# Attention of the first block in rounds of two units with four score banks, transposes in the dense banks

## The chip, the core and the metric

One core of a Trainium2 chip runs the whole program. The metric is the device time of one execution in microseconds (us), from the first to the last instruction and what lies around them.

## The reference

Two transformer blocks of two layers each work on a sequence of 512 positions and 1024 features, all in fp32. A layer of the first block does this:

```python
h = rmsnorm(x, norm_g[layer])
u = h @ w_in[layer]                       # split into q, k, v, gates of A, B, C
ya = forgetting_attention(qa, ka, va, log_sigmoid(fa + b)) * silu(za)   # 4 heads, causal, decay
yb = dilated_mixture_attention(rope(qb), rope(kb), vb) * silu(zb)       # 6 heads, 3 dilations
yc = banded_attention(rope(qc), rope(kc), vc, 127, sinks) * silu(zc)    # 6 heads, window 128
merged = sigmoid(ga)*(ya @ w_br_a) + sigmoid(gb)*(yb @ w_br_b) + sigmoid(gc)*(yc @ w_br_c)
x = x + merged @ w_out[layer]
```

The second block has a layer with differential attention under a relative position bias and a multi-scale pooling ("smoothing") branch, and one with a gated convolution. In each follow a cross attention to 256 memory positions and an MLP with a squared ReLU. A last rmsnorm ends the program.

## The kernel before

Everything is feature-major: x is kept as 8 tiles of 128 features by 512 positions. A dense product keeps fp32 accuracy by splitting each operand into a rounded high part and the rest: per group of 128 features, three fp32r matmuls (high by high, low by high, high by low; lines 333 to 335, and 359 to 361 or 881 to 883 where the positions are the stationary side). Eight groups are one gemm of 128 output features, and it fills one PSUM bank. Attention products (scores in line 534, values in line 622, transposes in line 602) are plain fp32 matmuls, scores and values on half of the array each for the two heads of a unit.

Weights come packed, 128 by 1024 for a gemm, through four raw buffers (`fetch`, line 201). ScalarE writes the high part (`round_hi`), VectorE the low part (`rest_lo`), which also issues the fetch four weights ahead. `ahead` keeps this two to three weights in front of the gemm.

The order on each engine is that in which the Python program emits operations. Generators yield after each group of a gemm. `drive(main, fill, num, den)` runs the attention of one kind as `main` and spreads the dense work of the next kind, `fill`, between its yields, num/den steps for each yield. `later(f, n)` puts a step off by n calls of `flush`.

A unit of attention is a pair of heads and one or two blocks of 128 queries. "forget" (A) has 6 units, "mix" (B) 9 and "sink" (C) 6 in each layer. In step i `attention` emits norm(i-1), values(i-2) and scores(i), yields, then turn(i-1), the transposes of the probabilities, and yields again. Scores take two PSUM banks (SB), transposes two others (PTP), values one (OB), dense gemms three (G). After the scores VectorE adds the bias and takes the maximum, ScalarE the exponential; `norm` divides by the sum on VectorE; after `turn` ScalarE copies the transposed tile to SBUF (PTb), from where `values` reads it.

At the start the first weight, the vector gv and x (four pieces of 512 KB) are loaded in that order; four squares of x for the norm are taken on GpSimd and four on ScalarE. `norm_end` and `stage` put the steps of a norm at given groups of the dense stream; evictions are held back until the last of them.

In the second block the relative bias is loaded from DRAM with a skew and then turned over by a product with a flip matrix (line 1145). Each pooling group has a weight chunk of its own. The cross attention is `cross`, its scores are line 1363, values line 1413 and transposes line 1389.

The driving calls of the first block are:

```python
drive(attention(units("forget", ...), gate_y(...)), gens_B(tokB), 98, 16)
drive(attention(units("mix", ...), gate_y(...)), gens_C(tokC), 138, 22)
drive(attention(units("sink", ...), gate_y(...)), gens_D(), 112, 16)
```

Of the kernel before, what the change touches and what calls it, by code (L numbers as in the profile page):

```python
# [14 lines left out]
NRAW, NHI, NLO, NTMP, NTMX = 4, 4, 3, 5, 5  # L15
# [126 lines left out]
def lay_out(nc, A, plan, T):  # L142
# [13 lines left out]
    PTS = Turns([T["PTb"][:, i, :] for i in range(2)])  # L156
# [44 lines left out]
    def fetch(j):  # L201
        if dry or j >= len(plan):
            return
        n = columns(plan[j])
        dst = raw[:, j % NRAW, 0:n]
        src = A["wts"][128 * offs[j]:128 * offs[j] + 128 * n].rearrange("(p f) -> p f", p=128)
        deps = [W["hi"][j - NRAW], W["lo"][j - NRAW]] if j >= NRAW else []
        W["raw"][j] = Q.dma(SP, lambda e: e.dma_start(dst, src), T["s_w"][j % NRAW],
                            16 * (j // NRAW + 1), *deps)
# [34 lines left out]
    class Weight:  # L244
        def __init__(self, c):
# [6 lines left out]
            self.tok = [W["hi"].get(i), W["lo"].get(i)]  # L252
# [7 lines left out]
        def done(self, o):  # L260
            W["done"][self.i] = o

    fetch(0)
    c_gv = load(gv[:, :], A["gv"])
    c_x = [load(X[:, 2 * i:2 * i + 2, :], A["xT"][:, 2 * i:2 * i + 2, :]) for i in range(4)]
    for j in range(1, NRAW):
        fetch(j)
    c_I = load(ident[:, :], A["ident"])
    c_sv = load(sv[:, :], A["sv"])
    c_tri = load(T["tri"][:, :], A["tri"])  # L270
    c_cos = load(T["cosT"][:, :], A["cosT"])
# [7 lines left out]
    round_hi(0)  # L279
    rest_lo(0)  # L280
    W["h"] = W["l"] = 1
# [41 lines left out]
    def gemm_fm(src, w, parts, evac, N=512, last=True, every=1, n0=0):  # L323
# [3 lines left out]
        for n, (b, t) in enumerate(parts):  # L327
# [9 lines left out]
            o = op(PE, f, w.tok if first else None, src.tok[t], free if first else None)  # L337
# [36 lines left out]
    def drive(main, fill, num, den):  # L374

        acc = 0
        for _ in main:
# [142 lines left out]
    def attention(units, done_pair, late_values=False):  # L520
# [73 lines left out]
        def turn(u):  # L594
            cols = u["cols"]
            u["PT"] = []
            for t, ready in u["P"]:
                bank, free = PTP.take()

# [9 lines left out]
                PTP.give(bank, a)  # L609
# [26 lines left out]
        st["clear"] = op(DV, lambda e: e.memset(T["ST"][:, :, 8:16], 1.0), [f for _, f in STT.idle if f])  # L636
        n = len(units)
# [47 lines left out]
    def to_rope(scale, dst, tok, key):  # L685
        def evac(bank, p):
# [23 lines left out]
            later(rest, 3)  # L710
# [100 lines left out]
    for m in range(8):  # L811
        h = op(AC, act(P0.hi[:, m, :], X[:, m, :], ACT.Copy, scale=gcol("norm0", m)), c_x[m // 2], c_gv)
        P0.tok[m] = [h, op(DV, stt(P0.lo[:, m, :], X[:, m, :], gcol("norm0", m), P0.hi[:, m, :].bitcast(F32),
                                   ALU.mult, ALU.subtract), h)]
    round_hi(1)
    rest_lo(1)
    W["h"] = W["l"] = 2
    for m in range(8):
        if m < 4:
            t, free = TMP.take()  # L820
            sq = op(PO, mult(t, X[:, m, :], X[:, m, :]), c_x[m // 2], free)
        else:
            t, sq = tmp_act_square(X[:, m, :], c_x[m // 2])
        sqa[1] = op(DV, (lambda e, t=t: e.tensor_copy(sqa[0], t)) if m == 0 else add(sqa[0], sqa[0], t), sq, sqa[1])
        TMP.give(t, sqa[1])

# [5 lines left out]
    for l in range(2):  # L832
        if l == 0:
            norm_end((15, 18, 19))
# [77 lines left out]
        def gens_A():  # L912
            yield from projections_A([(QA, qA, "q", 0), (KA, kA, "k", 0)])
            yield from values_A()
            steps = forget()
            rest = projections_A([(QA, qA, "q", 1), (KA, kA, "k", 1)])
            for n, _ in enumerate(rest):
# [6 lines left out]
        def gens_B(tok):  # L924
            for i in range(2):
                yield from gemm_fm(P0, WI(l, ZA + 128 * i), parts8(), to_silu(i, ztok))
# [57 lines left out]
        flush()  # L984
        tokB, tokC = {}, {}
        drive(attention(units("forget", tok, 2, qA, kA, vA), gate_y([0, 1], [0, 1], ztok)), gens_B(tokB), 98, 16)
        drain()
        drive(attention(units("mix", tokB, 3, qB, kB, vB), gate_y([2, 3, 4], [2, 3, 4], ztok)), gens_C(tokC), 138, 22)
        drain()
        drive(attention(units("sink", tokC, 3, qC, kC, vC), gate_y([5, 0, 1], [0, 1, 2], ztok)), gens_D(), 112, 16)  # L990
# [45 lines left out]
    assert len(TB.idle) == 3 and len(PTP.idle) == 2  # L1036
    OB.idle += PTP.idle[1:]
    PTP.idle = PTP.idle[:1]
# [26 lines left out]
    stage((6, one), (11, two), (13, three))  # L1065

    def prepare():
# [9 lines left out]
        lv, flip, oh, rel, frow = T["lvec"], T["flip"], T["oh"], T["rel"], T["frow"]  # L1077
# [3 lines left out]
        c_flip = load(flip[:, :], A["flip"], deps=[hrow])  # L1081
# [35 lines left out]
        c_fr = load(scr, frow[:, :], deps=ft)  # L1117
        yield
# [15 lines left out]
        K["mrow"] = spread(MRC[:, 0:2], K["mcol"], n=2, dst=MRB[:, :], B=SB)  # L1134
        yield
        cs = []
        for h in range(4):

            src = bass.AP(tensor=scr.tensor, offset=scr.offset + 640 * h, ap=[[1, 128], [1, 512]])
            cs.append(load(BI4[h], src, deps=[c_fr, K["sq2"], htok, K["mcol"]]))  # L1140
        for h in range(4):
            for _ in range(3):
                yield
            bank, free = SB.take()
# [3 lines left out]
            SB.give(bank, btok[h])  # L1148
# [73 lines left out]
    def mix(g):  # L1222
        w = Weight(chunk("pool_w", g, halves(0, 1), halves(0, 1)))

        def evac(bank, p):
            t, free = TMP.take()
# [629 lines left out]
```

How the kernel before makes its waits and increments, by code:

```python
    def dma(self, eng, fn, sem, val, *deps):  # L93
        self.op(eng, lambda e: fn(e).then_inc(sem, 16), *deps)
        return Landed(sem, val)
# [9 lines left out]
    def play(self, eng, e):  # L105
        seen = {}
        for o in self.of[eng]:
            need = {}
            for d in o.deps:
                v = need.get(id(d.sem), (0, None))[0]
                need[id(d.sem)] = (max(v, d.val), d.sem)
            for k, (v, s) in need.items():
                if seen.get(k, 0) < v:
                    e.wait_ge(s, v)
                    seen[k] = v
            ins = o.fn(e)
            if o.sig:
                ins.then_inc(o.sem, 1)
# [23 lines left out]
def lay_out(nc, A, plan, T):  # L142
# [1512 lines left out]
                o = send(0, *((0, 3), (3, 3), (6, 2))[m - 3])  # L1655
                if m == 5:
                    SB.give(end[0]["row"][0], o)
    mlp(1, n2)
    drain()
    last_norm(1)
    last_row(1)
    for m, n in ((0, 3), (3, 3), (6, 2)):
        send(1, m, n)
    op(SP, lambda e: e.wait_ge(T["s_o"], 16 * sent[0]))
    return Q, used
```

## Time and profile before

| | us |
|---|---|
| median of 3 runs (2334.63 to 2336.03) | 2334.96 |
| the profiled execution | 2335.33 |
| its span, first to last instruction | 2333.5 |
| TensorE busy | 2305.0 (99%) |
| VectorE busy | 1290.5 (55%) |
| ScalarE busy | 852.4 (37%) |

A matmul's end is modelled, and a busy TensorE is not one at its peak: how dense the stream is shows in the distance between the starts of neighbouring matmuls. Where an engine sits idle ahead of an instruction, the profile names what ended the wait.

### The profile page before, as it was taken

The numbers are of one execution on the slowest core, as the hardware profiler recorded it, in microseconds if no ns is written. First come the engines' busy times: TensorE is split into PE (matmuls) and PEld (weight loads), VectorE is DVE, ScalarE is ACT, GpSimd is POOL, SyncE is SP. The second block draws the span as 40 slices with busy tenths as digits, with TensorE's granted clock in tenths as the row PEclk, the third lists the DMA queues.
The fourth block names the chain that finished last, engine by engine and source line by source line (L and its number), as shares of the span: only waits on it lengthen the run. The fifth ranks groups of instructions, "written<-read, shape, count | busy, mean of one in ns | idle before, by whom it ended". The sixth has DMA issues, their size and how long they took to land.

```text
span 2333.5 us, 28447 instructions
## 1 busy us (share of the span) xinstructions
PE 2305.0 (99%) x11480; PEld 1876.6 (80%) x11480; DVE 1290.5 (55%) x2226; ACT 852.4 (37%) x1416; POOL 18.9 (1%) x18
## 2 busy tenths in 40 slices
PE   8999999999999999999999999999999999999998
PEld 6787778878777887878889888888888887888887
DVE  5855565557556556587545544444655546444445
ACT  4434443333344334255333432232322334332233
POOL 0000000000000000200000000000000000000000
PEclk9999999999999999999999999999999999999999
DMA  4322223323322233224224232323223212222321
GB/s 164 95 87 82 86 68 100 108 74 100 91 81 76 81 97 114 69 91 137 89 84 134 90 100 91 99 91 99 91 92 98 86 50 90 92 99 92 98 92 62
DMA packets 66408, 216.98 MB, mean 93 GB/s; under 512 B 8384, under 2 KB 11712, under 8 KB 66149
## 3 DMA queue, kind: packets, MB, share of 16 engines
q1 hardware_dynamic: 66276, 215.16, 28.9%
q8 instruction: 91, 1.49, 0.3%
q14 instruction: 41, 0.33, 0.0%
HBM read 207.78 MB, written 2.11 MB: 90 GB/s over the span
## 4 chain that ended last, share of the span: by engine, by line
PE 95%; DVE 3%; ACT 1%; POOL 0%; issue 0%; DMA 0%; POOLq 0%; DVEq 0%; SPq 0%; ACTq 0%
PE ps L333 27%; PE ps L335 27%; PE ps L334 27%; PE ps L534 2%; PE ps L622 2%; PE ps L359 2%; PE ps L360 2%; PE ps L361 2%; PE ps L602 2%; PE ps L1363 1%; PE ps L1413 1%; PE ps L423 1%; DVE t_wlo L171 1%; POOL t_UP L168 0%; DVE t_P0L L174 0%
## 5 line engine op out<-in xcount | busy, mean ns | idle before, releaser
L333 PE MATMUL ps<-t_P0H,t_whi 128*128 128x512 f32 x1664 | 672.7, 404 | 11.8 <-DVE t_P0L L174 9.6
L335 PE MATMUL ps<-t_P0H,t_wlo 128*128 128x512 f32 x1664 | 656.9, 395 | 0.0
L334 PE MATMUL ps<-t_P0L,t_whi 128*128 128x512 f32 x1664 | 655.9, 394 | 0.0
L180 ACT ACTIVATE t_whi<-t_raw 128x1024 fp32r<-128x1024 f32 (+3 forms) x396 | 404.6, 1026 | 383.6 <-PE ps L335 334.7
L171 DVE TENSOR_TENSOR t_wlo<-t_raw,t_whi 128x1024 fp32r<-128x1024 f32 (+3 forms) x395 | 466.9, 1185 | 12.3 <-ACT t_whi L180 7.3
L333 PEld LDWEIGHTS ps<-t_P0H,t_whi 128*128 128x128 f32 x1664 | 314.0, 189 | 105.1 <-issue 23.4
L335 PEld LDWEIGHTS ps<-t_P0H,t_wlo 128*128 128x128 f32 x1664 | 313.5, 188 | 73.2
L334 PEld LDWEIGHTS ps<-t_P0L,t_whi 128*128 128x128 f32 x1664 | 313.9, 189 | 69.7 <-issue 2.2
L333 PE MATMUL ps<-t_P1H,t_whi 128*128 128x512 f32 (+1 forms) x932 | 360.7, 387 | 1.7 <-DVE t_P1L L171 1.7
L334 PE MATMUL ps<-t_P1L,t_whi 128*128 128x512 f32 (+1 forms) x932 | 359.5, 386 | 0.0
L335 PE MATMUL ps<-t_P1H,t_wlo 128*128 128x512 f32 (+1 forms) x916 | 355.6, 388 | 0.0
L333 PEld LDWEIGHTS ps<-t_P1H,t_whi 128*128 128x128 f32 x932 | 175.6, 188 | 40.6 <-DVE t_P1L L171 2.5
L334 PEld LDWEIGHTS ps<-t_P1L,t_whi 128*128 128x128 f32 x932 | 175.3, 188 | 37.5
L335 PEld LDWEIGHTS ps<-t_P1H,t_wlo 128*128 128x128 f32 x916 | 172.1, 188 | 37.8
L168 DVE TENSOR_TENSOR t_X<-ps,t_X 128x512 f32<-128x512 f32 (+1 forms) x136 | 89.7, 659 | 159.1 <-PE ps L335 159.0
L180 ACT ACTIVATE t_TMP<-t_TMP 128x512 f32<-128x512 f32 x88 | 55.7, 633 | 293.2 <-DVE t_TMP L174 229.3
L174 DVE SCALAR_TENSOR_TENSOR t_TMP<-ps,t_RB 128x512 f32<-128x512 f32 x64 | 44.2, 691 | 178.4 <-PE ps L335 178.4
L180 ACT ACTIVATE t_Tb<-t_Tb,t_ST 128x256 f32<-128x256 f32 (+3 forms) x128 | 68.3, 534 | 154.7 <-DVE t_ST L177 154.5
L180 ACT ACTIVATE t_P0H<-t_X,t_gv 128x512 fp32r<-128x512 f32 x56 | 39.9, 723 | 143.9 <-DVE t_X L174 130.4
L174 DVE SCALAR_TENSOR_TENSOR t_X<-ps,t_X 128x512 f32<-128x512 f32 x48 | 33.2, 692 | 104.1 <-PE ps L335 104.1
L180 ACT ACTIVATE t_P1H<-t_TMP 128x512 fp32r<-128x512 f32 x88 | 55.7, 633 | 87.1 <-DVE t_TMP L165 47.7
L180 ACT ACTIVATE t_PTb<-ps 128x384 f32<-128x384 f32 (+1 forms) x112 | 55.4, 533 | 62.4 <-PE ps L602 40.2
(242 smaller groups left out, 2410.0 us busy)
## 6 DMA issues: line engine op xcount, KB each, us to landing
t_raw<-in_wts SPq DMA_DIRECT2D x364, 512.0 KB, 3.5
t_raw<-in_wts SPq DMA_DIRECT2D x16, 384.0 KB, 3.0
t_raw<-in_wts SPq DMA_DIRECT2D x4, 520.0 KB, 6.4
t_X<-in_xT SPq DMA_DIRECT2D x4, 512.0 KB, 7.4
t_raw<-in_wts SPq DMA_DIRECT2D x8, 256.0 KB, 2.6
t_TMX<-t_TMX SPq DMA_DIRECT2D x28, 64.0 KB, 2.0
t_TMP<-t_TMX SPq DMA_DIRECT2D x24, 64.0 KB, 2.0
outT<-t_X SPq DMA_DIRECT2D x4, 384.0 KB, 3.1
```

Source lines behind the costliest of these rows:

```text
L168: return lambda e: e.tensor_tensor(o, a, b, ALU.add)
L171: return lambda e: e.tensor_tensor(o, a, b, ALU.subtract)
L174: return lambda e: e.scalar_tensor_tensor(out=o, in0=a, scalar=s, in1=b, op0=f, op1=g)
L180: return lambda e: e.activation(o, a, f, **k)
L333: e.matmul(bank[:, 0:N], wh, xh, start=first, stop=False)
L334: e.matmul(bank[:, 0:N], wh, xl, start=False, stop=False)
L335: return e.matmul(bank[:, 0:N], wl, xh, start=False, stop=end)
L359: e.matmul(out, xh, wh, start=k == 0, stop=False)
L360: e.matmul(out, xh, wl, start=False, stop=False)
L361: return e.matmul(out, xl, wh, start=False, stop=k == 7)
L534: i = e.matmul(bank[:, o:o + n], l, r, start=True, stop=True)
L602: i = e.transpose(bank[:, j:j + 128], t[:, j:j + 128], ident[:, :])
```

## The change

Attention of the first block is emitted in rounds of two units: values of the last round, scores of both new units, two yields, then norm of each, and the transposes of each head as steps of their own. Scores have four banks, transposes use the dense banks, and the probabilities have two more buffers on either side of the transposes. If the second unit of the last round opens a new pair of heads, its values come after the scores.

```diff
-    G = Turns([ps[:, b, :] for b in (0, 1, 2)])
-    SB = Turns([ps[:, b, :] for b in (3, 4)])
-    PTP = Turns([ps[:, b, :] for b in (5, 7)])
-    OB = Turns([ps[:, 6, :]])
+    spare = [ps[:, b, :] for b in (6, 7)]
+    G = Turns([ps[:, b, :] for b in (0, 1, 2)] + spare)
+    SB = Turns([ps[:, b, :] for b in (3, 4, 5)])
+    PTP = Turns([])
+    OB = Turns([])
...
-        def turn(u):
+        def turn(u, which=None, B=PTP):
...
+        if in_rounds:
+            rounds = [units[i:i + 2] for i in range(0, len(units), 2)]
+            for r, now in enumerate(rounds + [[]]):
+                past = rounds[r - 1] if r else []
+                crossing = len(past) == 2 and past[1]["first"]
+                for u in past[:1] if crossing else past:
+                    values(u)
+                for u in now:
+                    scores(u)
+                if crossing:
+                    values(past[1])
+                yield
+                flush()
+                if now:
+                    yield
+                    flush()
+                for u in now:
+                    yield
+                    flush()
+                    norm(u)
+                for u in now:
+                    for j in range(2):
+                        yield
+                        flush()
+                        turn(u, j, G)
+            return
...
-            later(rest, 3)
+            later(rest, 4)
...
-        drive(attention(units("forget", tok, 2, qA, kA, vA), gate_y([0, 1], [0, 1], ztok)), gens_B(tokB), 98, 16)
+        drive(attention(units("forget", tok, 2, qA, kA, vA), gate_y([0, 1], [0, 1], ztok), in_rounds=True), gens_B(tokB), 90, 25)
```

"mix" is driven with 138, 38 and "sink" with 112, 25. Until the first layer's first projections are done the two spare banks serve dense gemms; then bank 6 becomes the output bank and bank 7 the fourth score bank. One gate gemm moves from the fill of "forget" to the projections ahead of it, and the second query projection ahead of the values.

At the beginning the first two weights are loaded and split in halves, x in eight pieces laid out one after the other, with the second half of the first weight behind the second piece. Eleven products of a matrix of ones run on TensorE first. All squares of x are taken on ScalarE, and the norm's steps come later:

```diff
+    def warm(e):
+        for _ in range(11):
+            i = e.matmul(ps[:, 4, 0:128], ones[:, :], ones[:, :], start=True, stop=True)
+        return i
+
+    op(PE, warm, c_ones)
+    split_cut(0, 0)
...
-            norm_end((15, 18, 19))
+            norm_end((19, 21, 23))
```

A weight's `done` now also calls `ahead`. In the second block the bias is copied 128 times in DRAM by DMA and read back with a skew that needs no flip; the row of the memory norm gets three yields between its two steps; the four pooling weights are one chunk, and a pooled product is split straight from PSUM:

```diff
+        c_rep = [load(A["rep"][h], scr[h:h + 1, :].broadcast_to([128, 640]), deps=[c_fr]) for h in range(4)]
...
-            p = op(PE, lambda e, bank=bank, h=h: e.matmul(bank, flip[:, :], BI4[h], start=True, stop=True),
-                   cs[h], c_flip, free)
-            btok[h] = op(DV, lambda e, bank=bank, h=h: e.tensor_copy(BI4[h], bank), p)
...
+            src = bass.AP(tensor=rep.tensor, offset=rep.offset + 128 * 640 * h + 127, ap=[[639, 128], [1, 512]])
+            btok[h] = load(BI4[h], src, deps=[c_rep[h], K["sq2"], htok, K["mcol"]])
```

`drive` has a new argument `lead`, fill steps taken ahead of the first step of `main`: two for the even attention (90, 42 in place of 92, 41) and for both cross attentions. The second cross attention waits five fill steps in place of three before it opens output gemms, and opens a third one, of six groups, before it ends the first two.

## Rows read from the trace of the kernel before

**Rows 1.** The page: busy us of each engine, and one group of VectorE's.
```profile
PE 2305.0 (99%) x11480; PEld 1876.6 (80%) x11480; DVE 1290.5 (55%) x2226; ACT 852.4 (37%) x1416; POOL 18.9 (1%) x18
...
L174 DVE SCALAR_TENSOR_TENSOR t_TMP<-ps,t_RB 128x512 f32<-128x512 f32 x64 | 44.2, 691 | 178.4 <-PE ps L335 178.4
```
**Rows 2.** Waits of TensorE, whole run: us, times, longest us.
```profile
PE ps L1363 <- DVE t_E L174: 2.5, 4, 0.8
PE ps L333 <- DVE t_wlo L171: 2.5, 2, 2.2
PE ps L333 <- DVE t_P1L L171: 1.7, 2, 1.4
```
**Rows 3.** Order of time, TensorE, scores alone: start, us, instruction.
```profile
63.97 0.40 PE L334 MATMUL ps<-t_P0L,t_whi 128*128 128x512 f32 x1
64.20 0.40 PE L335 MATMUL ps<-t_P0H,t_wlo 128*128 128x512 f32 x1
64.53 0.92 PE L534 MATMUL ps<-t_QKV 64*128 64x384 f32 x4
...
65.71 0.39 PE L334 MATMUL ps<-t_P0L,t_whi 128*128 128x512 f32 x1
```
**Rows 4.** Order of time, TensorE, values alone.
```profile
239.05 0.39 PE L335 MATMUL ps<-t_P0H,t_wlo 128*128 128x512 f32 x1
239.38 0.88 PE L622 MATMUL ps<-t_PTb,t_QKV 128*64 128x128 f32 x12
...
240.52 0.39 PE L334 MATMUL ps<-t_YL,t_whi 128*128 128x512 f32 x1
```
**Rows 5.** Order of time, TensorE, values and scores together.
```profile
85.29 0.39 PE L335 MATMUL ps<-t_P0H,t_wlo 128*128 128x512 f32 x1
85.61 0.88 PE L622 MATMUL ps<-t_PTb,t_QKV 128*64 128x128 f32 x12
86.41 0.93 PE L534 MATMUL ps<-t_QKV 64*128 64x128 f32 x8
...
87.62 0.39 PE L334 MATMUL ps<-t_P0L,t_whi 128*128 128x512 f32 x1
```
**Rows 6.** Order of time, TensorE, the first scores of layer 0.
```profile
54.36 1.68 PE L534 MATMUL ps<-t_QKV 64*128 64x128 f32 x8
```
**Rows 7.** Order of time, TensorE, transposes of two units.
```profile
69.63 0.82 PE L602 MATMUL ps<-t_ident,t_Tb 128*128 128x128 f32 x6
...
176.84 1.03 PE L602 MATMUL ps<-t_ident,t_Tb 128*128 128x128 f32 x8
```
**Rows 8.** Order of time, ScalarE, the copies of those transposes.
```profile
71.55 0.85 ACT L180 ACTIVATE t_PTb<-ps 128x384 f32<-128x384 f32 x2
...
177.48 1.09 ACT L180 ACTIVATE t_PTb<-ps 128x512 f32<-128x512 f32 x2 [1.13 <-PE ps L602]
```
**Rows 9.** Stretch of "forget": PE, PEld, DVE, ACT, POOL busy, PEclk, DMA share, GB/s.
```profile
54.00:131.00 77.00, 76.43 (x459) 61.27 (x460) 57.08 (x121) 29.66 (x60) 0.00 (x0) 1.00 0.30 89
```
**Rows 10.** Groups of VectorE, 53 to 125 us: count, busy us, mean ns.
```profile
L174 DVE SCALAR_TENSOR_TENSOR t_Tb<-ps,t_fg,t_M 128x512 f32<-128x512 f32 x3 | 2.2, 748 | 5.7 <-PE ps L534 5.7
```
**Rows 11.** Order of time, the start, all engines.
```profile
7.94 5.08 ACT L180 ACTIVATE t_P0H<-t_X,t_gv 128x512 fp32r<-128x512 f32 x8 [2.59 <-DMA t_X<-in_xT]
8.69 7.81 DVE L174 SCALAR_TENSOR_TENSOR t_P0L<-t_X,t_gv,t_P0H 128x512 fp32r<-128x512 f32 x8 [2.09 <-ACT t_P0H L180]
9.56 0.79 PE L333 MATMUL ps<-t_P0H,t_whi 128*128 128x512 f32 x1 [9.56 <-DVE t_P0L L174]
...
18.01 0.39 PE L333 MATMUL ps<-t_P0H,t_whi 128*128 128x512 f32 x1
```
**Rows 12.** Two stretches of the first gemms, columns as in rows 9.
```profile
9.50:14.90 5.40, 5.34 (x11) 3.32 (x12) 5.40 (x6) 5.40 (x9) 3.80 (x3) 1.00 1.03 407
15.20:20.00 4.80, 4.80 (x22) 3.89 (x21) 4.70 (x7) 3.09 (x5) 0.00 (x0) 1.00 0.94 331
```
**Rows 13.** Order of time, TensorE, one flip product.
```profile
947.93 1.02 PE L1145 MATMUL ps<-t_E,t_flip 128*128 128x512 f32 x2
```

More of the change, by code:

```diff
@@ L251, in __init__ @@
             ahead(i)
-            self.tok = [W["hi"].get(i), W["lo"].get(i)]
+            self.tok, self.late = [W["hi"].get(i), W["lo"].get(i)], {}
+            if i < NCUT and not dry:
+                self.tok, second = ([W["hi"][i][k], W["lo"][i][k]] for k in range(2))
+                self.late = {4: second}
         def hi(self, b, n=1):
@@ L372, in gemm_tm, with drive @@
             finish(bank, o, lambda bank, p, t0=t0: evac(t0, bank, p))
-    def drive(main, fill, num, den):
+    def drive(main, fill, num, den, lead=0):
         acc = 0
+        for _ in range(lead):
+            next(fill)
         for _ in main:
@@ L592, in norm @@
             STT.give(s, o[-1])
-        def turn(u):
+        def turn(u, which=None, B=PTP):
             cols = u["cols"]
-            u["PT"] = []
-            for t, ready in u["P"]:
-                bank, free = PTP.take()
+            u.setdefault("PT", [])
+            for t, ready in u["P"] if which is None else u["P"][which:which + 1]:
+                bank, free = B.take()
                 def f(e, t=t, bank=bank):
@@ L924, in gens_B @@
         def gens_B(tok):
[L925 to L926 removed]
+            yield from gemm_fm(P0, WI(l, ZA + 128), parts8(), to_silu(1, ztok))
             for i in range(3):
@@ L1063, in three @@
         N.row = spread_it(N.diag, dst=RB[:, :], B=SB)
-    stage((6, one), (11, two), (13, three))
+    stage((6, one), (12, two), (15, three))
     def prepare():
@@ L1242, in fill_E @@
         yield from queries(1)
+        w = Weight(tuple(("pool_w", g, (0, 64), (0, 64)) for g in range(4)))
         for g in (0, 2):
-            yield from mix(g)
-            yield from mix(g + 1)
+            yield from mix(w, g)
+            yield from mix(w, g + 1)
             yield from queries(2 + g // 2)
@@ L1296, in rest @@
             TMP.give(t, hs[h])
-        later(rest, 2)
+        later(rest, 3)
         return [o]
@@ L1302, in even_main @@
         yield from attention(eun, head_done, late_values=True)
-        for _ in range(3):
+        for _ in range(4):
             flush()
@@ L1459, in fill @@
                 return
-            for _ in range(3):
+            for _ in range(5):
                 yield
@@ L1472, in cross @@
         if l == 0:
-            drive(main(), fill(), 5, 1)
+            drive(main(), fill(), 5, 1, lead=2)
         else:
-            drive(main(), fill(), 13, 3)
+            drive(main(), fill(), 13, 3, lead=2)
+        if open_:
+            open_.append(wo(2))
+            for _ in range(6):
+                next(open_[2])
         for g in open_:
```

135 lines of the change are left out of this document (81 added, 54 removed).

## The prediction

> **What bounds the kernel now.** I read the busy shares first, then the list of what TensorE waited for, then the stretches, and only then single insertions in order of time. TensorE is busy 99% of the span [rows 1], so the kernel is a queue of matmuls. Waits that the profile can name are few: besides the first start there are 2.5 us each for a rounded weight and for projected queries, and 1.7 us for the last split attention tiles [rows 2]. A gain must therefore come from these waits, from the start, from matmuls that go away, or from time that "busy" hides. The last is there. A dense matmul follows the one before it every 0.23 us [rows 3], but where an attention step is pushed between two of them, the stream loses more than the step's own work. I measure an insertion from the start of the last dense matmul ahead of it to the start of the second one behind it, less two dense steps of 0.23 us. Scores alone cost 65.71 - 64.20 - 0.46 = 1.05 us [rows 3], values alone 240.52 - 239.05 - 0.46 = 1.01 us [rows 4], values and scores together 87.62 - 85.29 - 0.46 = 1.87 us [rows 5]. Together they are 0.19 us cheaper than apart. The rows show why: scores use the array as 64*128, values as 128*64, dense work and transposes as 128*128. Apart there are four changes of shape, together three, so I take a change to cost 0.19 us.
>
> **Rounds of two units.** A layer has 6, 9 and 6 units in its three attentions, and each attention makes two insertions of scores alone, n-2 of values with scores and two of values alone: 6 x 2 + 15 x 3 + 6 x 2 = 69 changes of shape. After, each attention has 3, 5 and 3 rounds: an opening pair of scores (2 changes), then values, values, scores, scores (3 changes, six times a layer), the crossing form values, scores, scores, values (4 changes, once in "forget" and once in "mix"), and values alone at the end (2). That is 6 + 18 + 8 + 6 = 38. Saved: 31 x 0.19 = 5.9 us a layer, 11.8 us in both. Transposes keep the dense shape; cutting each unit's into two insertions I cost at nothing. The first scores of a layer's "forget" lose time too: eight passes take 1.68 us there [rows 6] against 0.93 us elsewhere [rows 5], because the second score bank has just held a spread row that ScalarE still copies. With four banks the fresh one comes third. That gives 2 x 0.75 = 1.5 us.
>
> **What the rounds add.** Two waits, neither in the trace of before. First, turn(u1, 1) now stands directly ahead of the next round's values, with no fill between; ahead there were some six steps. Eight transposes are begun within some 0.8 us (1.03 with the tail of the last), one head's four in 0.40; with ScalarE free the first copy starts 177.48 - 176.84 = 0.64 us after the first transpose, and the two take 1.09 [rows 7, 8]. The second unit's values can thus start about 0.64 + 0.57 + 0.05 = 1.26 us after the transposes began. TensorE is there after 0.40 (transposes) + 0.19 (change) + 0.61 (first unit's values, 86.41 - 85.61 less a change) = 1.20. So with a free ScalarE the first unit's values just cover the copy. With ScalarE behind a weight rounding the copy came 71.55 - 69.63 = 1.92 us after the first transpose, 1.3 late [rows 7, 8]. Between 0 and 1.3 I take 0.3, nearer the prompt row, since the round's exponentials are over by then. Eight such borders a layer; the last round of "mix" has one unit and no cover: 1.26 - 0.59 + 0.3, about 0.95. Sum 2 x (8 x 0.3 + 0.95) = 6.7 us; ends 1.3 and 25. Values of the second unit in a crossing have two score insertions as cover and cost nothing; without that cover they would wait for VectorE's evacuation of the one output bank.
>
> Second, VectorE gets two units' score work in one piece while it is busy 57.08 of 77 us in "forget" [rows 9]. Adding the bias to a head of 512 columns takes 0.75 [rows 10]; with the maximum, of about that length, and the small steps I put a head at 1.9 and the four heads of a round at 7.5 us. Five yields of 3.6 dense steps (12.4 us) stand between the scores and the first transposes; meanwhile dense work with its rope steps brings VectorE some 0.6 us per us, by my estimate. 7.5 + 0.6 x 7.4 (up to the first norm) + 1.4 for that norm is 13.3, so the transposes are due 0 to 3 us before their data in the second round, where rope steps are densest. I take 1 us a layer, 2 us in all; ends 0 and 6. In "mix" and "sink" one step does what "forget" needs three for, and I take nothing. Dense banks: three, each turn takes one and gives it back behind a copy; a dense gemm of 5.5 us lies between an eviction and the bank's next need, so nothing, and 0.5 us per round if VectorE is late.
>
> Attention net: 11.8 + 1.5 - 6.7 - 2 = 4.6 us.
>
> **The start.** TensorE begins at 9.56 us and is through the first gemm at 18.01 [rows 11], though eight groups are 5.5 us of work. It is slow for three reasons: x arrives from 7.9 us on, in pieces of 512 KB behind a whole weight; the low parts take 7.81 / 8 = 0.98 us each while GpSimd squares beside them (0.69 for the like operation elsewhere [rows 1]); and 11 matmuls run in 5.4 us where later 22 run in 4.8 [rows 12]. The view grants 1.00 in both, but the steps say the lower of the two clocks, 1.2 GHz, up to about 15 us. The Trainium skill ("TensorE: Matmul & The Clock Gate", Part 1) has the idle array at 1.2 GHz, released by activity; 11 warm-up matmuls ahead of the data are what that asks for. The change brings the first x behind 0.3 MB instead of 0.6, warms the array and takes the squares off GpSimd. All of x still comes behind the same 2.6 MB: 1.5 MB after 7.9 us, at 407 GB/s [rows 12] by 11.6. Then one copy (5.08 / 8 = 0.63), one low part (0.7) and one group (0.7): the first gemm ends near 14.0, a gain of 4.0. Two more dense banks and the later norm steps should take 0.9 us of small waits in the first 30 us with them. Sum 4.9; ends 2.5 (low parts no faster) and 6.5. ScalarE takes four more squares, 2.1 us, behind the copies, hidden by the second gemm; bare they would delay the norm row.
>
> **The rest.** The four flip products leave. The two passes of one last 1.02 us [rows 13] with the tail that the next matmul overlaps (a dense one lasts 0.40 and is followed after 0.23, so the tail is 0.17): 0.86 of the stream each, 3.4 us in all. The memory row's diagonal is built three yields earlier; I put the wait that this takes away at 0.7, about one VectorE step of that width [rows 1]. Together 4.1, ends 3 and 5. In their place four replicating transfers of 328 KB and four skewed loads run some 35 us ahead of their use. SP holds the weight fetches back while the bias row lands, by my estimate 2 us; raw weights lie more than two gemms ahead, so nothing, 2 us if that cover were gone. One pool weight instead of four small ones and two fill steps ahead: the 2.2 us wait for wlo goes [rows 2]; around it lie shorter waits and slow steps that I estimate at 1.3: 3.5, ends 1 and 4.5. Cross attention: two steps of lead take the waits for queries, 2.5 [rows 2], and a third output gemm covers most of the 1.7 for the split tiles; about 3.5 (ends 2 and 4.5).
>
> **Sum.** 4.6 + 4.9 + 4.1 + 3.5 + 3.5 = 20.6 us off the profiled execution's 2335.3 is 2314.7; the median of the runs is 0.4 lower: **2314 us**.
>
> **Rivals.** (a) The borders don't wait: ScalarE always ready, no burst: 6.7 - 1.3 + 2 = 7 us better, 2307. For it: the copy and the cover are equal to 0.06 us. Against it: ScalarE rounds a weight of 1 us per gemm. (b) The borders wait in full, 0.8 us each and VectorE 3 us a layer: 2 x (8 x 0.5 + 2) = 12 worse, near 2326. (c) The burst decides: VectorE, not TensorE, sets each round. If its two-unit piece makes the first transposes of all 22 rounds 2 us late, that is 44 us against 29 won (the sum without the two waits): 2335 + 15 = 2350, slower. It decides from 1.3 us per round, mean of all. For it: 74% busy in "forget"; against it: 55% over the span [rows 9, 1]. (d) The clock falls again: the groups of the first gemm come every 0.7 to 1 us, so TensorE is partly idle behind the warm-up; at 3 x 5.4 / 11 = 1.47 us a group [rows 12], from 6 us on, the gemm would end at 17.8, 3.8 later than I have it, and the time be 2318. The same page of the Trainium skill has idle gaps bring the low clock back; no row here shows it for gaps that short. (e) The change doesn't act: small waits eat each gain and it stays within 2330 to 2339.
>
> **Numbers.** Own forecast 0.49, (a) 0.14, (b) 0.18, (c) 0.07, (d) 0.07, (e) 0.05. What can be told from no change is about 0.2%, 4.7 us. Faster is all but (c) and (e): 0.88; same 0.05; slower 0.07. The range leaves out (c), (e) and the far ends: 2304 to 2326.
>
> **What would show it.** Attention stretches without the change of clock, score rows of two units in one piece, fewer changes of shape; a wait of TensorE for ScalarE's PTb copy at values, some 0.3 us, 1 at the end of "mix"; the first dense matmul near 6 us and the second gemm near 14; no flip rows; no wait for wlo near 1000 us. Wrong if the values or transposes wait over 1.3 us per round, or if the second gemm starts after 16 us.

## The result and the profile after

The changed kernel takes 2317.1 us (median of 4 runs, 2315.8 to 2318.2) beside 2334.9 us of the kernel before on the same chip: ratio 0.9923, 95% interval 0.9905 to 0.9940, a gain of 17.8 us where 20.6 had been worked out. Its profiled execution took 2317.4 us with a span of 2315.6. TensorE is still busy 99%. The page's busy line and the rows of its list of waits on which the text rests (columns as in [rows 2]):

```profile
PE 2292.8 (99%) x11494; PEld 1882.9 (81%) x11494; DVE 1282.3 (55%) x2217; ACT 859.4 (37%) x1419; POOL 13.9 (1%) x14
```

```profile
PE ps L661 <- ACT t_PTb L182: 4.2, 3, 2.4
PE ps L641 <- DVE t_QKV L176: 2.4, 2, 1.2
PE ps L661 <- ACT t_PTX L182: 1.8, 2, 1.0
PE ps L641 <- DVE t_Tb L176: 1.8, 3, 0.8
...
PE ps L641 <- DVE t_Tb L179: 1.0, 2, 0.5
```

The waits of [rows 2] are gone: none for projected queries, none for wlo, 0.3 us left for the split tiles. New ones stand in their place, at values (L661) and transposes (L641). (t_Tb holds the normalised probabilities, t_PTb and t_PTX their transposed copies; t_PTX is the two buffers that the change adds, all of them behind the transposes.)

Busy TensorE hides where time goes, so I lay the two traces side by side by dense matmuls. Both kernels issue the same 9708 of them; the time at which the n-th starts in the one, less that in the other, is how far the changed kernel is ahead. The gain of each stage, in us, for this kernel and for the experiments told below (each from one profiled execution, against the kernel before). The column "predicted" has the prediction's terms put into the stages: half of the attention net in each layer, and the 0.9 us of small waits in layer 0.

| stage, up to dense matmul | predicted | after | a_old_order | b_no_warm | c_pool_squares | d_border | e_turn_sb | f_spread | g_no_lead | h_all | i_border_spread | j_best | k_flips | l_flips_early |
|---|---|---|---|---|---|---|---|---|---|---|---|---|---|---|
| first gemm, 25th | 4.0 | 3.9 | 3.0 | 3.1 | 0.7 | 3.6 | 3.5 | 3.9 | 3.6 | 3.7 | 1.4 | 4.3 | 1.5 | 1.4 |
| layer 0, 1400th | 3.2 | 3.8 | 2.7 | 3.7 | 3.8 | 5.9 | 5.1 | 3.8 | 3.7 | 3.9 | 4.4 | 7.4 | 3.8 | 3.8 |
| layer 1, 3400th | 2.3 | 1.9 | 0.9 | 1.9 | 1.9 | 4.2 | 3.3 | 1.8 | 1.9 | 2.2 | 2.6 | 5.7 | 2.0 | 1.9 |
| bias and memory row, 3900th | 4.1 | 3.7 | 3.7 | 3.7 | 3.7 | 3.7 | 3.7 | 3.7 | 3.7 | 3.7 | 3.7 | 3.7 | -8.2 | 0.3 |
| even block's attention, 4600th | 3.5 | -1.1 | -1.1 | -1.1 | 0.5 | 0.5 | -1.1 | 1.7 | 0.5 | 1.7 | 0.2 | 1.7 | -1.1 | -0.9 |
| cross attentions, to the end | 3.5 | 5.2 | 5.1 | 5.1 | 5.2 | 5.1 | 5.1 | 5.2 | 1.6 | 5.2 | 5.0 | 5.1 | 5.1 | 5.2 |

A stage that an edit doesn't touch repeats within some 0.2 us from kernel to kernel, apart from the first gemm and the even block's attention, which the text comes to. So the table tells parts apart that are smaller than the spread of whole runs. Five of the six stages are near the prediction or better; the even block's attention is 4.6 us short of it, more than the 3.2 us that the sum lacks.

**The start** answers to [rows 11, 12]: TensorE in order of time, the 22 small matmuls of the warm-up (11 products in two passes), the first dense matmul, a wait for a low part, and the 25th dense matmul; then the stretch of [rows 12] again.

```profile
1.31 5.06 PE L314 MATMUL ps<-t_ones 128*128 128x128 f32 x22 [1.31 <-DVE t_nst L310]
7.15 0.50 PE L370 MATMUL ps<-t_P0H,t_whi 128*128 128x512 f32 x1 [0.77 <-ACT t_P0H L182]
...
9.81 0.50 PE L370 MATMUL ps<-t_P0H,t_whi 128*128 128x512 f32 x1 [0.86 <-DVE t_P0L L176]
...
14.12 0.39 PE L370 MATMUL ps<-t_P0H,t_whi 128*128 128x512 f32 x1
```

```profile
9.50:14.90 5.40, 5.08 (x22) 4.09 (x23) 5.31 (x10) 5.34 (x10) 0.00 (x0) 1.00 1.06 400
```

22 matmuls stand where 11 did, and from the first dense matmul on the steps between matmuls without a wait are 0.23 to 0.34 us, where the kernel before needs 0.43 and more.

**The rounds.** Where they wait: the transposes of the first round of "forget", and the last values of "mix" and "sink" in layer 0.

```profile
69.02 0.52 PE L641 MATMUL ps<-t_ident,t_Tb 128*128 128x128 f32 x3 [0.54 <-DVE t_Tb L179]
...
72.78 0.55 PE L641 MATMUL ps<-t_ident,t_Tb 128*128 128x128 f32 x3 [1.15 <-DVE t_QKV L176]
...
249.41 1.09 PE L661 MATMUL ps<-t_PTb,t_QKV 128*64 128x128 f32 x16 [1.04 <-ACT t_PTb L182]
...
342.05 1.09 PE L661 MATMUL ps<-t_PTb,t_QKV 128*64 128x128 f32 x16 [0.73 <-ACT t_PTb L182]
```

And an ordinary border in "mix", where the prediction had put 0.3 us between the two units' values:

```profile
156.10 0.49 PE L641 MATMUL ps<-t_ident,t_TbX 128*128 128x128 f32 x3
156.52 0.88 PE L661 MATMUL ps<-t_PTb,t_QKV 128*64 128x128 f32 x12
157.23 0.82 PE L661 MATMUL ps<-t_PTX,t_QKV 128*64 128x128 f32 x12
157.99 1.89 PE L573 MATMUL ps<-t_QKV 64*128 64x512 f32 x12
```

The second values start 0.71 us after the first, which is the twelve passes' own time: no wait. The waits are few and long, not many and short. The list of waits gives 2.4 + 1.0 + 1.8 + 1.8 = 7.0 us for both layers (the 2.4 us one at L661 belongs to the even block).

**The even block's attention** is where the forecast failed. TensorE in order of time, then ScalarE and VectorE just before:

```profile
1006.09 0.40 PE L372 MATMUL ps<-t_P0H,t_wlo 128*128 128x512 f32 x1
1008.89 0.94 PE L661 MATMUL ps<-t_PTb,t_E 128*128 128x128 f32 x6 [2.40 <-ACT t_PTb L182]
...
1010.99 0.63 PE L370 MATMUL ps<-t_P0H,t_whi 128*128 128x512 f32 x1
1011.41 0.63 PE L371 MATMUL ps<-t_P0L,t_whi 128*128 128x512 f32 x1
```

```profile
1004.90 1.06 ACT L182 ACTIVATE t_whi<-t_raw 128x1024 fp32r<-128x1024 f32 x1
1007.83 0.63 ACT L182 ACTIVATE t_TMP<-t_E 128x512 f32<-128x512 f32 x1 [1.87 <-DVE t_E L1363]
1008.37 0.47 ACT L182 ACTIVATE t_PTb<-ps 128x384 f32<-128x384 f32 x1
```

```profile
1003.52 0.75 DVE L176 SCALAR_TENSOR_TENSOR t_P1L<-ps,t_gv,t_P1H 128x512 fp32r<-128x512 f32 x1 [1.35 <-ACT t_P1H L182]
1004.18 1.22 DVE L173 TENSOR_TENSOR t_wlo<-t_raw,t_whi 128x1024 fp32r<-128x1024 f32 x1
1005.32 0.74 DVE L176 SCALAR_TENSOR_TENSOR t_P1L<-ps,t_gv,t_P1H 128x512 fp32r<-128x512 f32 x1
1005.98 1.22 DVE L173 TENSOR_TENSOR t_wlo<-t_raw,t_whi 128x1024 fp32r<-128x1024 f32 x1
1007.11 0.68 DVE L1363 COPY t_E<-ps 128x512 f32<-128x512 f32 x1
```

Read backwards: the values wait for ScalarE's copy of the transposes (1008.37); that stands in ScalarE's queue behind a head's square (1007.83), which waits 1.87 us for VectorE's copy of the head (1007.11); and that stands behind two weight roundings and two split tiles. So the pool mixes still bring a burst on. Before, it was wlo that came late, by 2.2 us [rows 2], in a VectorE queue that was full too, though of attention's steps more than of roundings: wlo stood behind a norm (from 998.90 on), the score work of a unit and an eviction.

```profile
998.90 0.18 DVE L577 RECIPROCAL t_ST<-t_ST 128x4 f32<-128x4 f32 x1 [0.78 <-ACT t_Tb L180]
...
1001.84 0.68 DVE L174 SCALAR_TENSOR_TENSOR t_E<-ps,t_RB 128x512 f32<-128x512 f32 x1
1002.43 1.22 DVE L171 TENSOR_TENSOR t_wlo<-t_raw,t_whi 128x1024 fp32r<-128x1024 f32 x1
```

Now roundings and splits hold up an innocent copy for 2.4. Behind it the steps are 0.43 us instead of 0.23, and the row of the stretch shows the clock granted at the lower of its two levels, 1.2 GHz, most of the time (0.57 in the PEclk column; columns as in [rows 9]):

```profile
1010.00:1012.40 2.40, 2.40 (x8) 1.42 (x6) 1.45 (x6) 1.94 (x5) 0.00 (x0) 0.57 0.16 63
```

### The profile page after: what moved, and what is told of

It is laid out like the page before. It is cut to its first block, busy times and chain, and to the rows that moved or that the text cites. A ratio compares the mean times of both kernels' runs of the same rounds, so it can differ in the third digit from the quotient of the medians.

```text
span 2315.6 us, 28450 instructions
## 1 busy us (share of the span) xinstructions
PE 2292.8 (99%) x11494; PEld 1882.9 (81%) x11494; DVE 1282.3 (55%) x2217; ACT 859.4 (37%) x1419; POOL 13.9 (1%) x14
## 4 chain that ended last, share of the span: by engine, by line
PE 94%; DVE 3%; ACT 1%; POOL 0%; issue 0%; DMA 0%; SPq 0%; POOLq 0%; DVEq 0%; ACTq 0%
PE ps L370 27%; PE ps L372 27%; PE ps L371 26%; PE ps L661 2%; PE ps L573 2%; PE ps L396 2%; PE ps L397 2%; PE ps L398 2%; PE ps L641 1%; PE ps L1485 1%; PE ps L1435 1%; PE ps L462 1%; POOL t_UP L170 0%; DVE t_wlo L173 0%; PE ps L948 0%
## 5 line engine op out<-in xcount | busy, mean ns | idle before, releaser
L176 DVE SCALAR_TENSOR_TENSOR t_TMP<-ps,t_RB 128x512 f32<-128x512 f32 x64 | 44.3, 691 | 178.7 <-PE ps L372 178.7
L176 DVE SCALAR_TENSOR_TENSOR t_X<-ps,t_X 128x512 f32<-128x512 f32 x48 | 33.2, 691 | 100.3 <-PE ps L372 100.3
L167 DVE TENSOR_TENSOR t_TMP<-ps,t_RB 128x512 f32<-128x512 f32 x34 | 23.5, 692 | 93.7 <-PE ps L372 93.7
```

Source lines behind the costliest of these rows:

```text
L176: return lambda e: e.scalar_tensor_tensor(out=o, in0=a, scalar=s, in1=b, op0=f, op1=g)
```

## The experiments

All times are medians in us beside 2317.1 of the changed kernel; the kernel before ran beside each (2333.97 to 2335.6). Kernels are called by the first letter of their names where that is plain. An experiment's own runs spread by 0.6 to 5 us, so differences under 2 us are read from the table of stages.

### What the rounds are worth: a_old_order

```
-        if in_rounds:
+        if in_rounds and False:
             rounds = [units[i:i + 2] ...
```
(with the two transpose banks, two score banks and the shares 16, 22 and 16 of the kernel before)

> The change with its first block's attention put back: units one after another, transposes in the two banks of before, two score banks, the old shares of dense work; all else as after. My theory (an array-shape change costs 0.15 to 0.2 us, so the rounds are worth about 1.9 us in each of the two layers at equal dense work): about 3.7 us slower than after, 2320.8 us, with nothing else moved by more than 0.5 us. Rival: the rounds are worth nothing net, since their own waits of 4.0 us a layer eat the saving, and layer 0's gain comes from the earlier start: 2317 us. Rival: the prediction's count of 4.6 us net for both layers: 2321.7 us.

Measured: 2319.7 (2317.9 to 2320.7; ratio to before 0.9935, 0.9922 to 0.9947). That is 2.6 more than with the rounds, but the two intervals overlap; the stages are clearer: 2.7 instead of 3.8 in layer 0, 0.9 instead of 1.9 in layer 1, nothing elsewhere but 0.9 in the first gemm, which the edit doesn't touch (its matmuls went at half rate from 8.7 us on). So the rounds are worth 1.0 to 1.1 us a layer, some 2.1 in all: less than half of the 4.6 forecast and less than my 3.7, which had put down to them 0.9 us a layer that the kernel in the old order has too.

### Waits at the ends of "mix" and "sink": d_border

```
+                if past:
+                    yield
+                    flush()
                 for u in past[:1] if crossing else past:
                     values(u)
```
(shares 28, 43 and 28 instead of 25, 38 and 25)

> The change with one more group of dense products put at each border of two rounds, ahead of the first unit's values (the shares of dense work raised to 28, 43 and 28 so that the amount in each stretch stays). My theory: only three waits a layer are left there (the end of the second stretch and of the third, about 1.0 us each), so some 2 to 4 us in all, 2313 to 2315 us, unless each extra split of a merged run costs two changes of array shape (0.15 us each, 8 borders, two layers: 4.8 us), which would eat it: 2317 to 2319 us. Rival of the prediction: the border waits are the full 6.7 us, so 2310.5 us.

Measured: 2312.9 (2311.6 to 2316.0; ratio 0.9909, 0.9895 to 0.9922). The waits at values in the first block are down to two of 0.3 us, and each layer gains 2.1 to 2.3 us more. But the wait in front of the first transposes of each layer has grown, from 0.5 us to 1.9:

```profile
PE ps L641 <- DVE t_Tb L179: 3.8, 2, 1.9
```

The reason is in the stretch before it; VectorE (third of the busy columns) is full, TensorE is not:

```profile
60.00:69.00 9.00, 7.41 (x33) 5.67 (x31) 8.65 (x21) 5.72 (x15) 0.00 (x0) 1.00 0.17 60
```

But VectorE's share is 8.65 of these 9 us in the changed kernel too, where TensorE has 8.48. What differs is the dense work. The first scores and the first transposes of the layer, in the changed kernel (whose transposes start at 69.02, above) and in d:

```profile
54.10 1.67 PE L573 MATMUL ps<-t_QKV 64*128 64x128 f32 x12
```

```profile
54.41 1.67 PE L573 MATMUL ps<-t_QKV 64*128 64x128 f32 x12
...
69.34 0.52 PE L641 MATMUL ps<-t_ident,t_Tb 128*128 128x128 f32 x3 [1.93 <-DVE t_Tb L179]
```

The chain through VectorE takes 14.9 us in both. A share of 28 in place of 25 hands out fewer dense groups for each yield, so that 48 dense matmuls stand in these 14.9 us in place of 54: 6 x 0.23 = 1.4 us less cover, which is what the wait has grown by. The group at the border was taken out of a stretch that had none to spare.

### Waits of the transposes for a dense bank: e_turn_sb

```
-                        turn(u, j, G)
+                        turn(u, j, SB)
```

> The change with the transposes of the first block written to the score banks, not to the dense ones. Theory: the waits of 1.1 to 1.3 us at the first transposes of a layer are for VectorE's eviction of a dense bank, so they go: 2.4 us faster, about 2314.7 us. Rival: VectorE is late there anyway (the transposes' input, the normalised tile, is 0.5 to 0.7 us late in the turn before), so the wait only changes its name: 2317 us. Second rival: the score banks are now held by the transposes until ScalarE's copy, the first scores of the next round wait at each border (16 borders, up to 0.5 us each): up to 8 us slower, 2325 us.

Measured: 2315.1 (2314.3 to 2315.4; ratio 0.9916, 0.9903 to 0.9930), 1.4 us more in each layer. The wait at L641 for t_QKV (2.4 us, the eviction of a dense bank) is gone, that for t_Tb L179 is unchanged at 1.0, and no score waits in its place. A transpose that borrows a dense bank waits for that bank's eviction; the score banks were free when the transposes came.

### The burst of roundings: f_spread

```
-            yield from mix(w, g)
-            yield from mix(w, g + 1)
-            yield from queries(2 + g // 2)
+            for g in (2 * i - 4, 2 * i - 3):
+                yield from mix(w, g)
+                for _ in range(4):
+                    next(q)
+                    yield
+            yield from q
```

> The change with the pool mixes of the first even block spread: four groups of the queries' dense products between one mix and the next, so that the smoothing's roundings do not come in one burst on VectorE and ScalarE. Theory: the wait of 2.4 us of the values for the copy of the transposes, and the half-rate products behind it (about 10 steps, 0.2 us more each), are due to the burst of weight roundings: they go, 2.4 to 3.5 us faster, 2313.9 to 2314.9 us. Rival: the burst only moves to the next rounding that a product needs, and a wait of 1 us or more stands there under the name of the weight: 2316 to 2318 us.

Measured: 2315.1 (2314.8 to 2315.4; ratio 0.9917, 0.9903 to 0.9930); the even block's stage goes from -1.1 to 1.7. The wait of 2.4 us for the copy is gone, and the matmuls behind it keep their 0.23 us. As the rival had it, part of the wait stands elsewhere, here for a split of a pooled product (the matmul does not read t_P1L; the split is straight from PSUM and gives the bank back):

```profile
1012.65 0.39 PE L370 MATMUL ps<-t_MH,t_whi 128*128 128x256 f32 x1 [0.79 <-DVE t_P1L L176]
```

### Warm-up: b_no_warm

```
-    op(PE, warm, c_ones)
```

> The change without the 11 products of ones ahead of the first dense product. Prediction's step: half-rate steps of 0.43 us come back from 9.56 on as in the kernel before, some 4 us of them (the second product's start at 18.0 instead of 14.1), so 2321 us. Rival: the first products are now paced by the arrival of the input's pieces (0.67 us apart) and the smaller vector work, not by the clock, and half-rate steps hide in that: less than 1 us, 2317 to 2318 us.

Measured: 2317.5 (2316.5 to 2318.4; ratio 0.9929, 0.9914 to 0.9944). The half-rate steps do come back, but only seven of them (the last at 10.5 us), and they stand where the kernel with the warm-up waits for low parts; the first gemm ends 0.8 us later. The rival was right.

```profile
7.77 0.80 PE L369 MATMUL ps<-t_P0H,t_whi 128*128 128x512 f32 x1 [7.77 <-DVE t_P0L L176]
8.37 0.63 PE L370 MATMUL ps<-t_P0L,t_whi 128*128 128x512 f32 x1
...
11.46 0.39 PE L369 MATMUL ps<-t_P0H,t_whi 128*128 128x512 f32 x1
```

### Squares beside the low parts: c_pool_squares

```
+        if m < 4:
+            t, free = TMP.take()
+            sq = op(PO, mult(t, X[:, m, :], X[:, m, :]), c_x[m], free)
+        else:
             t, sq = tmp_act_square(X[:, m, :], c_x[m])
```

> The change with the squares of the first four pieces of the input on GpSimd again. Theory: they stretch VectorE's subtractions for the low parts beside them (0.98 us each before, 0.68 after); P0L of these pieces comes up to 0.3 us later each, the second product's start 0.5 to 1.2 us later: 2317.6 to 2318.3 us. Rival: the pieces arrive 0.67 us apart and bind, so no change, 2317.1 us.

Measured: 2319.4 (2317.6 to 2321.8; ratio 0.9938, 0.9922 to 0.9955), and the first gemm loses 3.2 of its 3.9 us: more than either theory gave. GpSimd's squares stretch VectorE's work beside them, a low part from 0.74 to as much as 1.52 us and a weight's low part from 0.69 to 1.52; TensorE, at half rate from its fourth matmul on, runs dry ahead of 11.70. That matmul, the first of the third group, starts at 9.81 in the changed kernel: 1.9 of the 3.2 us are lost by then, to the late low part. The other 1.3 are lost behind it, where the steps are 0.43 us until 14.4; they are the clock's, and as the text on the start tells below, the clock was low there in executions without GpSimd's squares too.

```profile
5.71 5.38 POOL L167 TENSOR_TENSOR t_TMP<-t_X 128x512 f32<-128x512 f32 x4 [5.27 <-DMA t_X<-in_xT]
...
6.49 2.26 DVE L176 SCALAR_TENSOR_TENSOR t_P0L<-t_X,t_gv,t_P0H 128x512 fp32r<-128x512 f32 x2 [1.70 <-ACT t_P0H L182]
...
8.67 1.52 DVE L173 TENSOR_TENSOR t_wlo<-t_raw,t_whi 128x512 fp32r<-128x512 f32 x1
...
11.70 0.80 PE L370 MATMUL ps<-t_P0H,t_whi 128*128 128x512 f32 x1 [1.24 <-DVE t_P0L L176]
```

The Trainium skill ("SBUF — State Buffer", "SBUF: two separate sides") says that a GpSimd operation that reads SBUF and a VectorE operation with two inputs in SBUF take a common port pair in turns, and that the loser stands still for the whole of the other's instruction. The rows agree: both stretched operations read two tiles in SBUF, and the 0.83 us that the weight's low part lost is less than one square of 5.38 / 4 = 1.35.

### The lead of the cross attentions: g_no_lead

```
-            drive(main(), fill(), 5, 1, lead=2)
+            drive(main(), fill(), 5, 1)
```
(and the same in the second)

> The change with the two cross attentions' dense work handed out without the two groups of lead. My theory from the trace (the weight waits at the start of each cross stretch are gone since the lead): 2 to 3.5 us slower, 2319 to 2320.5 us, all of it between the even attention's end and the cross attention's end. Rival: the third output product alone covers the waits, and the lead is worth under 0.5 us: 2317 to 2317.6 us.

Measured: 2320.7 (2320.1 to 2322.2; ratio 0.9944, 0.9929 to 0.9958), 3.6 more. The last stages give 1.6 instead of 5.2, and the waits for projected queries are back, with L1435 the scores:

```profile
PE ps L1435 <- DVE t_E L176: 3.2, 4, 1.5
```

### The flip products: k_flips and l_flips_early

```
+        for h in range(4):
+            for _ in range(3):
+                yield
+            bank, free = SB.take()
+            p = op(PE, lambda e, bank=bank, h=h: e.matmul(bank, flip[:, :], BI4[h], start=True, stop=True), cs[h], c_flip, free)
+            btok[h] = op(DV, lambda e, bank=bank, h=h: e.tensor_copy(BI4[h], bank), p)
```
(the four loads of the bias from the small table, instead of the replicating and skewed transfers, are issued behind the memory row in k_flips, and three steps earlier, behind its diagonal, in l_flips_early)

> The change with the bias's four flip products on TensorE and their loads as before, instead of the skewed loads; the memory row's earlier diagonal stays. The prediction's count: four products of 0.86 us of the stream, 3.4 us: 2320.5 us. Rival: the whole 4.2 us that the trace shows between the two layers and the even attention are theirs: 2321.3 us. Rival: the products only fill time that other waits leave, so less than 1 us: 2318 us.

Measured: 2329.7 (2328.3 to 2331.8; ratio 0.9980, 0.9971 to 0.9989). I had not put the flips back as they were: the loads went out at 942.17, behind two weight fetches on the same queue, where the first product was due, and it waited.

```profile
948.08 2.05 PE L1223 MATMUL ps<-t_E,t_flip 128*128 128x512 f32 x2 [6.11 <-DMA t_E<-scr]
```

With the half-rate matmuls behind it this one wait cost more than the products: the stage fell by 11.9 us. So the second kernel:

> The flip products once more, but with their four loads issued three steps earlier, right behind the memory row's diagonal and ahead of the weight fetches that stood before them in the kernel with the flips put back (there the first product waited 6.1 us for its load). Theory: without the wait the flips cost their own four insertions of 0.86 us of the stream: 3.4 us, 2320.5 us. Rival: the loads land late in any place, since the queue of the weights is full there: a wait of some us stays, 2323 us or more.

Measured: 2320.7 (2319.0 to 2323.5; ratio 0.9935, 0.9921 to 0.9948). No wait, and the stage gives 0.3 instead of 3.7: the four products are worth 3.4 us, as forecast, and the memory row's earlier diagonal 0.3, not 0.7.

```profile
941.92 1.02 PE L1223 MATMUL ps<-t_E,t_flip 128*128 128x512 f32 x2
```

### Do the cures add up: h_all, i_border_spread, j_best

h_all has the edits of d, e and f together (shares 26, 43 and 27), i_border_spread those of d and f.

> The three additions together: a dense group at each border of two rounds, transposes in the score banks, pool mixes spread; shares 26, 43 and 27 so that the first turn of a layer has more dense work ahead of it. If they add up (4.3, 2.0 and 2.0 us by the medians): 2308.8 us; with the first turn's wait of 1.9 us a layer in the bordered kernel cut by half as well: 2307 us. Rival: the score banks, held by the transposes, make the first scores wait at the borders now that values come after them: 2311 to 2313 us.

Measured: 2314.7 (2313.9 to 2314.7; ratio 0.9916, 0.9901 to 0.9931), no better than d alone (2312.9), and behind it in both layers. Layer 0 gains no more than after, layer 1 0.3 more. TensorE's waits are back at the transposes, twice a layer:

```profile
PE ps L641 <- DVE t_Tb L179: 5.5, 4, 1.6
```

The 1.2 us one of a layer's two stands at the first transposes, as in d; the longer one stands in the second round, and its cause is open.

> The dense group at each border and the spread mixes, transposes in the dense banks. Theory: the three additions failed to add up because in the first stretch ('forget') VectorE sets the pace: every wait taken away there comes back in front of a transpose as a wait for the normalised tile (5.5 us in the kernel with all three). The border and the spread act in different stages, so these two add up: 4.3 and 2.0 off 2317.1, 2310.8 us. Rival: the sum is bounded elsewhere (what one gains is lost in the even attention or behind it): 2313 us or more.

Measured: 2314.2, in two groups (2312.4 and 2312.5; 2316.0 and 2317.4; ratio 0.9916, 0.9902 to 0.9929); the profiled one is the longest. It has the same wait as d in front of the same transposes, 1.92 and 1.93 us, yet here the clock fell behind it, to 0.61 of full, and in d it did not:

```profile
71.48 0.52 PE L641 MATMUL ps<-t_ident,t_Tb 128*128 128x128 f32 x3 [1.92 <-DVE t_Tb L179]
```

```profile
71.40:75.00 3.60, 3.52 (x12) 2.82 (x13) 3.53 (x9) 1.44 (x2) 0.00 (x0) 0.61 0.47 147
```

The same stretch in d, behind its wait that ended at 69.34:

```profile
69.30:73.00 3.70, 3.66 (x19) 3.11 (x20) 3.63 (x10) 1.94 (x3) 0.00 (x0) 1.00 0.36 125
```

So neither of the two theories is settled by the median; the two short executions, of which there is no profile, come to 2312.4, 1.6 above the sum of the parts. The stages of the long one speak for the sum: it lies 2.2, 1.6 and 1.6 us behind d in the first gemm and the two layers and 1.5 behind f in the even block, at each of these places with more matmuls at half rate, and 2317.4 less these 6.9 is 2310.5 (an estimate from the table), where the sum of the parts was 2310.8.

j_best puts the border group only where VectorE has room (condition `past[0]["kind"] != "forget"`; shares 25, 43 and 28, so that the first stretch keeps its 54 dense matmuls), and has the edits of e and f.

> Transposes in the score banks, spread mixes, and the dense group at the borders in the second and third stretch only ('mix', 'sink'); the first stretch keeps its 25 shares. Theory (VectorE sets the pace in 'forget', so nothing is to be forced there): 2.0 + 2.0 as measured singly, and about 2 us a layer of border waits in the other two stretches: 2317.1 - 8 = 2309 us. Rival: with transposes in the score banks the borders of 'mix' and 'sink' wait for those banks: 2312 to 2314 us.

Measured: 2307.5 (2306.8 to 2308.8; ratio 0.9887, 0.9872 to 0.9902): 9.6 us less than the changed kernel, and the two intervals don't meet. No wait at values is left anywhere in its list, the wait for the dense bank is gone, and the one for t_Tb L179 is 1.0 as after. The layers gain 7.4 and 5.7 us. The end of "mix", which had waited at 249.41, and the even block's stretch:

```profile
246.42 1.09 PE L661 MATMUL ps<-t_PTb,t_QKV 128*64 128x128 f32 x16
```

```profile
1010.00:1012.40 2.40, 2.40 (x24) 2.40 (x23) 2.29 (x11) 0.89 (x3) 0.00 (x0) 1.00 0.68 205
```

## Why the prediction was right, and where its terms were off

The time lay 3.1 us from the forecast and inside the range, but by terms whose errors partly cancel.

**Attention net, 4.6 forecast, 2.1 measured** (a_old_order). With the 7.0 us of waits in the trace the rounds save 9.1 before them; less 1.5 for the first scores (the twelve matmuls of two units take 1.67 us at 54.10, where the eight of one unit took 1.68 [rows 6]) that is 7.6 for 62 changes of shape, 0.12 each and not 0.19. Where the missing 0.07 goes is open. It is not the transposes cut in two, which the prediction put at nothing: by its own measure of an insertion, eight in one piece cost 0.87 us in the kernel before and four cost 0.44 in the changed one (means over both layers).

**The two waits** came to 7.0 where 6.7 + 2 had been put, but at other places. The eight borders a layer cost nothing [rows 7, 8 gave 0 to 1.3 us]: the first unit's values do cover the copy. The last round of "mix" waits 1.04 (forecast 0.95), and so does that of "sink" with 0.73, which the forecast had not listed since it has two units. VectorE's burst makes the transposes 0.5 us late a layer, not 1: the prediction had their data 13.3 us behind the scores, and they came 69.02 - 55.70 = 13.3 us behind the scores' end. The dense bank, costed at nothing since a gemm lies between (with 0.5 us per round if VectorE is late), costs 1.2 us a layer in that same round.

**Rival (c), VectorE's burst**, is refuted for the kernel as it is, but it is the fence next to it. In the first round of "forget" the chain through VectorE takes 14.9 us from the first scores to the first transposes, in the changed kernel, d, e, h, i and j alike, and the changed kernel covers all but 0.5 of them. Where dense work moves from there to a border (48 matmuls left in d and i, 51 in h, of 54), the wait grows, to 1.9 us in d and i and 1.2 in h. That is why the cures don't add up there, and why j leaves that stretch alone.

**The start, 4.9 forecast.** The first gemm gained 3.9 (forecast 4.0, though the terms that the prediction names for its end, 11.6 + 0.63 + 0.7 + 0.7, come to 13.6 and not to 14.0). The remaining 2.7 of layer 0 in the old order are more than the 0.9 I gave to small waits. Waits of 0.7 us (L881) and 0.4 (L423) that the list of the kernel before names there are gone; the rest, and the 0.9 of layer 1 in the old order, for which the prediction has no term, I have not split up. Of the reasons named for the first gemm, the squares off GpSimd carry 1.9 us by their late low part (c), the warm-up at most 0.8 (b); no run takes back the earlier and smaller pieces of x. And rival (d), the clock falling again after the warm-up, is not refuted by the one profile in which it doesn't: of the twelve profiled executions with a warm-up, d, g, i, k and l began their dense matmuls at half rate, and a and c fell to it soon after. Where it lasted over five microseconds (i, k, l) the first gemm lost 2.4 to 2.5 us (they also began some 1 us late, but e, as late and at full rate, lost 0.4); where it ended by 11 us (d, g) it hid in the wait for low parts and cost 0.3.

**Bias and memory row, 4.1 forecast, 3.7 measured**: 3.4 for the flips as forecast, 0.3 for the rest of the stage, which I put down to the row (l).

**Even block's attention, 3.5 forecast, -1.1 measured: the step that failed.** "The 2.2 us wait for wlo goes", and it went; but I priced the wait and did not ask what made wlo late. Two pool mixes in a row bring two roundings of 1.04 to 1.22 us on both vector engines, with two split tiles among them, and one wide weight instead of four small ones doesn't shorten that. The burst found the next thing in the queues, the copy of the transposes, for 2.4 us, and the clock fell behind it as it had before (matmuls 0.43 us apart from 1005.9 to 1008.2 in the kernel before). f shows the cause: the same roundings with four groups between the mixes bring 2.8 us back. In c, d and g the same 2.4 us wait was not followed by half-rate steps there, and their stage is 1.6 us better: that is what the clock alone costs here. So of f's 2.8 us 1.2 are the wait and 1.6 the clock behind it. The other 1.8 of the 4.6 that are missing stay open; 1.1 may be the waits of transposes for t_Tb L176, which rose in this stage from 0.7 us to the 1.8 of the list, in f too. No run takes back the one wide weight or the two steps of lead.

**Cross attention, 3.5 forecast, 5.2 measured**: 3.6 by the lead (g), where the waits for queries by name were 2.5 [rows 2]; what stands beside a named wait came on top. The 1.6 that stay without the lead are close to the 1.4 by which the wait for split tiles shrank (1.7 to 0.3); that the third output gemm did this is not shown, since no run takes it away.

## What to carry to other kernels

A wait on the list names the operation that was last in a crowded queue; taking that operation away moves the wait to its neighbour unless the crowd is spread, so price the burst and not the name. When TensorE is the bound, gains in one stage add up only as long as the other engines have room in that same stage. Where another engine's chain takes a fixed time between two insertions (14.9 us here), count the matmuls that cover it in each kernel: dense work that is moved out of that stretch to cover a wait elsewhere comes back as a wait of its own length. Lay two traces side by side by the count of the work that both must do; it resolves tenths of a microsecond where medians can't tell two.

## What the runs showed of the hardware

- The granted clock after a wait of TensorE is not the same from run to run: behind waits of 1.92 and 1.93 us at the same instruction it was 0.61 (i) and 1.00 (d), behind 2.4 us in the even block it fell in the changed kernel and stayed full in d, and behind the 0.8 us for the split of a pooled product it fell in i (0.66 in the 4 us that follow) and not in f. Each fall cost about 1.5 us more. That may be why the runs of d and i spread by 4 to 5 us and those of j by 2, but e has the 2.4 us wait and spreads by 1.1, so it is not shown.
- At the beginning the page's PEclk shows 1.00 through 9.5 to 14.9 us in the kernel before [rows 12], though the steps are at half rate; there the distance between matmuls is the better reading.
- Four GpSimd squares of 1.35 us, which TensorE never waits for, made its third group 1.9 us late, by way of VectorE (c). The medians differ by 2.3 us, but the runs overlap, and the clock has a part in it.
- Five of twelve profiled executions with 5.06 us of warm-up matmuls began their dense matmuls at half rate, by the distance between them, and two more fell to it soon after (a, c).
